# Positions of gathered rows dealt over groups of 8 partitions, and gathered rows turned by VectorE from the eleventh block on, in a mixture-of-experts decoder step

## The reference, cut to what matters

```python
T = 576; D_MODEL = 1024; N_EXPERTS = 64; TOP_K = 8; D_EXPERT = 256
s = sigmoid(h @ w_router); ...            # group-limited choice of 8 experts for each token
def step(acc, blk):                       # one block: up to 128 tokens
    e, tok, wt = blk
    xb = h[tok]
    hb = silu(xb @ we_g[e]) * (xb @ we_u[e])
    return acc.at[tok].add(wt[:, None] * (hb @ we_d[e]))
```

## Time and profile before

| | |
|---|---|
| median of 3 runs | 1124.86 us (1123.6 to 1125.34) |
| profiled execution, its own time | 1125.71 us |
| its span, first to last instruction | 1123.9 us |
| TensorE busy | 1092.7 us, 97% of the span |
| VectorE busy | 463.5 us, 41% |
| ScalarE busy | 236.7 us, 21% |
| GpSimd busy | 135.3 us, 12% |
| moved by DMA | 337.16 MB, mean 300 GB/s |

### The profile page before, as it was taken

One profiled execution on the slowest core, in us unless ns is written; L12 is line 12 of the kernel. 1 busy time (PEld: TensorE's weight loads), 2 busy tenths in 40 slices (PEclk: granted clock), 3 DMA queues, 4 the chain that ended last, 5 costly groups with the idle time before them and its releaser, 6 DMA issues.

```text
span 1123.9 us, 16923 instructions
## 1 busy us (share of the span) xinstructions
PE 1092.7 (97%) x6443; PEld 574.4 (51%) x6443; DVE 463.5 (41%) x1286; ACT 236.7 (21%) x516; POOL 135.3 (12%) x163
## 2 busy tenths in 40 slices
PE   6999999999999999999999999999999999999986
PEld 3456677777877544754343443443444444343332
DVE  2218541565456645843275233233233232231157
ACT  4131241223133223211111111111111111111111
POOL 0210000000020010121111112112111111111100
PEclk9999999999999999999999999999999999999999
DMA  9857622021170286789999999999999999999698
GB/s 371 325 201 302 227 79 75 1 85 34 80 255 18 91 286 229 273 302 403 418 425 424 423 417 426 422 415 398 424 411 379 422 408 392 415 395 370 222 415 341
DMA packets 51654, 337.16 MB, mean 300 GB/s; under 512 B 9636, under 2 KB 14088, under 8 KB 30830
## 3 DMA queue, kind: packets, MB, share of 16 engines
q1 hardware_dynamic: 33710, 287.32, 63.4%
q0 software_dynamic: 17856, 48.68, 11.7%
HBM read 311.30 MB, written 37.24 MB: 310 GB/s over the span
## 4 chain that ended last, share of the span: by engine, by line
PE 91%; DMA 4%; DVE 2%; ACT 1%; issue 1%; SPq 0%; DVEq 0%; POOLq 0%; ACTq 0%
PE bank L1565 30%; PE bank L1588 15%; PE bank L1261 10%; PE bank L1280 5%; PE bank L1553 4%; DMA mem<-expert_out_rows 3%; PE bank L1379 3%; PE bank L1174 3%; PE bank L1380 3%; PE bank L1497 3%; PE bank L1258 3%; PE bank L1149 1%; PE bank L1576 1%; PE bank L1344 1%; PE bank L1158 1%; PE bank L1132 1%
## 5 line engine op out<-in xcount | busy, mean ns | idle before, releaser
L1565 PE MATMUL bank<-mem 128*32 128x512 f32 (+2 forms) x1504 | 318.8, 594 | 0.6 <-DVE mem L2251 0.6
L1565 PEld LDWEIGHTS bank<-mem 128*32 128x32 f32 (+2 forms) x1504 | 106.7, 127 | 194.2 <-issue 194.2
L1588 PE MATMUL bank<-mem 128*32 128x512 f32 (+2 forms) x752 | 164.2, 596 | 1.1 <-ACT mem L1069 1.1
L2251 DVE COPY mem<-bank 128x512 f32<-128x512 f32 x48 | 33.2, 692 | 283.3 <-PE bank L1553 283.3
L1261 PE MATMUL bank<-hT,mem 128*128 128x288 f32 x512 | 133.3, 409 | 1.0 <-ACT mem L939 1.0
L1261 PEld LDWEIGHTS bank<-hT,mem 128*128 128x128 f32 x512 | 93.8, 190 | 25.8 <-issue 2.4
L1565 PE MATMUL bank<-x_sb,mem 128*32 128x512 f32 (+2 forms) x400 | 105.8, 593 | 0.0
L1588 PEld LDWEIGHTS bank<-mem 128*32 128x32 f32 (+2 forms) x752 | 51.7, 127 | 72.0 <-issue 71.1
L1069 ACT ACTIVATE mem<-bank 128x256 f32<-128x256 f32 x48 | 18.4, 384 | 313.0 <-PE bank L1576 312.8
L2266 DVE COPY hT<-bank 128x512 f32<-128x512 f32 x48 | 33.2, 692 | 85.4 <-PE bank L1588 85.4
L794 POOL DMA_INDIRECT mem<-ffn_in_rows,idxg x32 | 32.9, 1028 | 264.7 <-DVE idxs L2247 211.0
(11 more groups left out here) (400 smaller groups left out, 1279.3 us busy)
## 6 DMA issues: line engine op xcount, KB each, us to landing
mem<-k_w_exp SPq DMA_DIRECT2D x52, 2048.0 KB, 19.3
mem<-in_w_exp_down SPq DMA_DIRECT2D x52, 1024.0 KB, 20.6
x_sb<-k_w_exp SPq DMA_DIRECT2D x12, 2048.0 KB, 23.8
mem<-k_w_ada SPq DMA_DIRECT2D x8, 2048.0 KB, 9.3
mem<-k_w_in SPq DMA_DIRECT2D x7, 2048.0 KB, 9.4
hT<-in_w_exp_down SPq DMA_DIRECT2D x12, 1024.0 KB, 22.2
mem<-expert_out_rows SPq DMA_DIRECT2D x6, 2048.0 KB, 16.5
mem<-k_w_head SPq DMA_DIRECT2D x4, 2048.0 KB, 18.4
```

The lines of the kernel that those rows point to most:

```text
L1565: i = mm(bank[sl, :], xT[:, j % 2, c * BLK + sl.start:c * BLK + sl.stop], wview(r)[0][:, c, :], start=c == 0, stop=c == KC - 1)
L1588: i = mm(ps[4 + hf][sl, :], hhT[:, k * BLK + sl.start:k * BLK + sl.stop], wview(r)[1][:, k, hf * 512:(hf + 1) * 512], start=k == 0, stop=k ...
```

## The change

Two things change, and the order of some work with them.

**Dealing.** `deal` is a small table, written once, in place of `iota` in `slots_of`. For an expert part of k quarters (32k slots, 4k groups of 8 partitions) the position p goes to group p mod 4k, so that consecutive positions lie 8 slots apart, and the empty slots are the last of each group of 8 and no longer the end of the part. This holds for all blocks.

**Turning.** From block 10 on (the eleventh), TensorE's 8 transposes `x_T` and the two copies `xT_evac` go. VectorE transposes instead from the gathered rows in SBUF straight into `xT`, in 16 instructions for a block: each takes 32 partitions and 8 pieces of 32 columns and transposes each 32x32 square. 38 blocks (10 to 47) are turned in this way.

**Order.** From b = 9 on, `hh_T(b-1)` stands between the sixth and the seventh chunk of `up(b)` (so far only for b = 47). `up`, the gathers and some final waits ask for the semaphore `xT_ready`, which VectorE raises after its copy or its last transpose.

```diff
@@ slots_of (VectorE)
-                return stt(pm, p.to_broadcast([P, NT, w]), off, iota[:, 0:w].unsqueeze(1).to_broadcast([P, NT, w]),
+                return stt(pm, p.to_broadcast([P, NT, w]), off, dealt(w // QS).unsqueeze(1).to_broadcast([P, NT, w]),
                            ALU.add, ALU.is_equal)
@@ set-up (VectorE), DR = 8
+            for k in range(1, P // QS + 1):
+                cp(dealt(k).rearrange("p (e r) -> p e r", r=DR), iota[:, 0:k * QS].rearrange("p (r e) -> p e r", r=DR))
@@ VectorE
+            def turn(n, j, s=None):
+                g = gbuf(n, j)
+                dve.wait_ge(S[f"gat{g}"], gcount(n, j, s))
+                dve.wait_ge(S["eup"], n - 1)
+                rows = xg[g].rearrange("s (c d) -> s c d", c=KC)
+                cols = xT[:, j % 2, :].rearrange("d (c s) -> d c s", c=KC)
+                for q in range(P // QS):
+                    for a in range(P // QS):
+                        sl, dl = slice(q * QS, (q + 1) * QS), slice(a * QS, (a + 1) * QS)
+                        i = dve.transpose(cols[dl, :, sl], rows[sl, :, dl])
+                i.then_inc(S["xT_ready"], 1)
...
             for b in range(NBK):
                 if b + XG < NBK:
                     place(b + XG)
-                if b < NBK - 1:
+                if b + 1 < TURNED:
                     xT_evac(b + 1, b + 1)
+                elif b + 1 < NBK:
+                    turn(b + 1, b + 1)
                 gated(b, b)
@@ TensorE, TURNED = 10
-                if b < NBK - 1:
-                    up(b, b, pieces(b))
-                else:
-                    up(b, b, pieces(b), range(KC - 2))
+                split = KC if b + 1 < TURNED else KC - 2
+                up(b, b, pieces(b), range(split))
                 if b == 0:
                     pe.wait_ge(S["tab_ready"], 1)
                 else:
                     hh_T(b - 1)
-                if b == NBK - 1:
-                    up(b, b, pieces(b), range(KC - 2, KC))
-                if b < NBK - 1:
-                    x_T(b + 1, b + 1)
+                if split < KC:
+                    up(b, b, pieces(b), range(split, KC))
+                if b + 1 < TURNED:
+                    x_T(b + 1)
@@ GpSimd, before a gather
-                    pool.wait_ge(S["xgT_t"], n - XG + 1)
+                    pool.wait_ge(S["xT_ready"], n - XG + 1)
```

More of the change, by code:

```diff
@@ L39 @@
 QS = 32
+DR = 8
 NPRE = 3
@@ L50 @@
 XG = 3
+TURNED = 10
 OVMAX = 4 * U
@@ L192, in build @@
         n_out = sb("n_out", [(1 + NB) * H, DH])
+        deal = sb("deal", [P, 10 * QS], BF16)
         wtab = sb("wtab", [P, RQ])
@@ L488, in dn_count, with dealt @@
             return DN_LOADED[slot(r)][1] + 16 * loads_of(r)
+        def dealt(k):
+            return deal[:, k * (k - 1) // 2 * QS:k * (k + 1) // 2 * QS]
         def load_down(sp, dn, d, s):
@@ L649, in _ @@
             sp.wait_ge(S["eup"], max(LASTB[r] for r in range(NE) if slot(r) == XSLOT) + 1)
-            sp.wait_ge(S["xgT_t"], NBK)
+            sp.wait_ge(S["xT_ready"], NBK)
             for t in range(NT):
@@ L670, in _ @@
             overflow(sp, nov, body, last=last_rows)
-            sp.wait_ge(S["xgT_a"], NBK)
-            sp.wait_ge(S["xgT_d"], NBK)
+            sp.wait_ge(S["xT_ready"], NBK)
             for k in range(2):
@@ L1078, in body @@
                 silu(n, j)
-                xT_evac(n + 1, j + 1)
                 hhT_evac(n)
@@ L1097, in _ @@
             out_rows(NBK - 1, NBK - 1)
-            overflow(act, nov, body, lambda: xT_evac(NBK, NBK))
+            overflow(act, nov, body)
             for i, (t, _) in enumerate(COMBINE):
@@ L1541, in find_idx, with x_T @@
                 i.then_inc(S["idx_mm"], 1)
[L1543 to L1547, removed]
+            def x_T(n):
+                g = gbuf(n, n)
+                pe.wait_ge(S[f"gat{g}"], gcount(n, n))
+                if n:
                     pe.wait_ge(S["xgT_a"], n)
-                    pe.wait_ge(S["xgT_d"], n)
+                    pe.wait_ge(S["xT_ready"], n)
                 else:
@@ L1556, in up @@
             def up(n, j, parts, cs=range(KC)):
-                pe.wait_ge(S["xgT_a"], n + 1)
-                pe.wait_ge(S["xgT_d"], n + 1)
+                if isinstance(n, int) and n < TURNED:
+                    pe.wait_ge(S["xgT_a"], n + 1)
+                pe.wait_ge(S["xT_ready"], n + 1)
                 if not (isinstance(n, int) and n < 2):
@@ L1605, in body @@
                 up(n, j, whole)
-                x_T(n + 1, j + 1, s + 1)
                 find_idx(n + 2, j + 2, whole)
@@ L1620, in _ @@
             shared_up(KC // 2)
-            x_T(0, 0)
+            x_T(0)
             shared_up(2)
@@ L1651, in first_blocks @@
                 find_idx(NBK, NBK, whole)
-                x_T(NBK, 0, 0)
                 find_idx(NBK + 1, NBK + 1, whole)
             def last_done():
-                pe.wait_ge(S["xgT_a"], nov + (NBK + 1))
-                pe.wait_ge(S["xgT_d"], nov + (NBK + 1))
+                pe.wait_ge(S["xT_ready"], nov + (NBK + 1))
                 pe.wait_ge(S["ehh"], nov + NBK)
@@ L1665, in _ @@
             overflow(pe, nov, body, first_blocks, last_done)
-            for name in ("xgT_a", "xgT_d", "ehh", "ehT", "eout_a", "eout_d", "idx_ready"):
+            for name in ("xT_ready", "ehh", "ehT", "eout_a", "eout_d", "idx_ready"):
                 pe.wait_ge(S[name], NBK)
@@ L2270, in body @@
                 gated(n, j)
-                xT_evac(n + 1, j + 1)
+                turn(n + 1, j + 1, s + 1)
                 idx_out(n + 2, j + 2, s + 2)
@@ L2306, in first_blocks @@
                 place_more(NBK + 1, NBK + 1, 1)
-                xT_evac(NBK, NBK)
+                turn(NBK, 0, 0)
                 idx_out(NBK + 1, NBK + 1)
```

11 lines of the change are left out of this document (5 added, 6 removed).

## The result

The changed kernel takes 1134.45 us (median of 4 runs, 1133.96 to 1136.84), and before takes 1124.49 (4 runs, 1123.60 to 1125.34): ratio 1.0093, interval 1.0075 to 1.0110. It is 10 us slower. The forecast was 1123.5, and the range ended at 1131. The profiled execution took 1136.84 us, with a span of 1135.0.

The account below looks back on a forecast made before the run. TensorE, 97% busy, was taken to bound the kernel, with the DMA engines nearly full beside it. From 1124.86: -2 kept after loads give back most of -27.4, dealing 0, +0.6 for waits, giving 1123.5 us; range 1106 to 1131.

Parts of the forecast that it names:

- TensorE's list: Expert stage, blocks 10 to 47: TensorE loses `x_T`, its list 27.4 us shorter, 0.72 us a block.
- The term for the split of `hh_T`: `hh_T` in the middle of `up` costs TensorE 0.25 us a block, 9.5 us over 38 blocks.
- What the loads give back: Expert stage: TensorE soon waits for weight loads, so only 0 to -7 us of its gain is kept; -2 taken.
- Turning on VectorE: VectorE's 16 transposes a block take 0.40 us each, 6.4 us together, hidden within the block.
- Rival C: Turned blocks: VectorE becomes the bound if a transpose costs over 0.53 us; 1169 us at 0.6, 1224 at 0.69; chance 0.10.
- Gathers, GpSimd and the four copies: Gathers land in time, GpSimd waits for the turning instead, four small table copies are hidden: nothing added.
- Dealing: Expert stage: the new slot order acts only through the DMA engines, between +3 and -25 us; 0 taken.
- The sentence on the Trainium skill's swizzle: Partitions go to 16 DMA engines in runs of four, so dealt empty slots would all fall to every other engine.
- Crowding, +0.6: Waits that move gathers and loads against each other add about 0.6 us.
- rival D, +4: Expert stage: stops for loads, a lower clock behind some and more fully loaded engines cost +4 us, 1129; chance 0.13.
- Rival B, 1104,: Expert stage: dealing levels the DMA engines and loads land sooner, 21 us gained, 1104 us; chance 0.17.

Follow-up runs that it names:

- experiment 7: Changed kernel with the second half of each down-projection load left out from the twelfth expert on: 1099.07 us, 0.9770 of before.
- experiment 2: Kernel before with only the turning by VectorE from the eleventh block on, positions in their old order: 1128.77 us, 1.0031 of before.
- experiments 3, 5 and 11: Changed kernel with dealing over groups of 4 (1113.14 us); dealing over 8 turned round by 4 every second block (1111.66); no dealing, every second block reversed (1109.78).
- experiment 1: Kernel before with only the dealing over groups of 8, all blocks still turned by TensorE: 1133.68 us, 1.0089 of before.
- experiment 9: Changed kernel with unread matmuls (2, 5, 9, 6 and 9) ahead of the waits of blocks 17, 21, 33, 40 and 46: 1133.83 us, 1.0077 of before.
- Experiment 12: Changed kernel with the deal over 8 turned round by 4 in all blocks from the 25th on: 1120.11 us, 0.9956 of before.

## Why the prediction was wrong

**TensorE's list: right.** Predicted -27.4 us for 38 blocks, 0.72 each, 11.26 us a block. Measured 0.79 each, 11.13 a block (experiment 7), -29.3 in 37 blocks. The term for the split of `hh_T` was too large: `up` and `hh_T` take 811.73 - 804.45 = 7.28 us in block 27, against 7.19, 0.09 more and not 0.25; over the 37 blocks the 0.79 leave 0.97 - 0.79 = 0.18 on average.

**What the loads give back: the mechanism right, the sign and size wrong.** I wrote that TensorE begins to wait some four blocks into the turned ones, and that between 0 and 7 us are kept, and took 2. The first stop behind block 10's is at block 17, 2.4 us long, and the stops sum to 29.0. But it was wrong that the term can't be above 0. Turning alone costs +3.5 us (experiment 2): the loads did not land when they landed before. In this run's stage they move 407 GB/s, as the kernel before does:

```profile
600.00:1046.00 446.00, 423.88 (x2811) 153.04 (x2805) 362.68 (x940) 50.53 (x111) 74.69 (x73) 0.97 0.99 407
```

In before TensorE waits for nothing, so its 407 is what TensorE asked for. Here TensorE asks earlier and waits 22.1 us, and gets no more; with the engines level it gets 418 to 421 (experiments 3, 5 and 11).

**Turning on VectorE: right.** I took 0.40 us; it is 0.436, and it is hidden. Rival C is out. (Its times were a little high by its own terms: 13.1 - 11.98 = 1.12 us a block and not 1.15, so 1167.5 and not 1169, and 1222 and not 1224.) Gathers, GpSimd and the four copies were costed at nothing, and with half the down bytes gone (experiment 7) nothing else stops TensorE.

**Dealing: this is the step that failed.** I bounded it between +3 and -25 and took 0, "since a group of 8 keeps its full slots together at its start". The +3 was worked out from no row. It costs 10 us alone (1.0089, experiment 1) and about 7 on top of the turning (1.0093 against 1.0031). The sentence on the Trainium skill's swizzle had the right mechanism: by that rule the empty slots all fall to every other engine. I let it stand beside the sum and not in it, and I judged the damage by "the rest would be as loaded as the worst is now". The counts say that too: the fullest engine has 375 rows of the stage against 369 before. What changed is how many are that full: eight have 368 to 375 rows, against three above 345 before. The landing of the same pair of loads went from 18.5 to 26.1 us.

**Crowding, +0.6, and rival D, +4.** D named three things: stops, a lower clock behind them, and engines as loaded as the worst. The first and the last hold, the middle one was a small cost of its own if any, and the price was under half of the +10. By the rows the clock looks expensive. The blocks behind the five stops are longer than the same blocks of experiment 7 by 10.0 us in all, and the account closes: -29.3 of list, +29.0 of stops, and 10 of clock make the +10 of block 47's start. Yet experiment 9 gave the clock back at all five of them (it lost it again behind the new stop) and the time moved by 1.8 us (1.0077 for 1.0093), 5 at the most by the ends of the intervals. An account that adds up is not a cause: as far as this goes, the clock mostly decided how the waiting was divided. As the fillers may have cost time themselves, its price is bounded only loosely.

**Rival B, 1104,** was what dealing would have brought if it had evened the engines. With a deal that does, the gain is 12 to 15 us (1109.78 to 1113.14), and not 21.

So in order: TensorE's shorter list makes the loads the bound, and with unequal engines they land late. From 600 to the start of the last block the kernel with turning alone moves 404 GB/s in 450.2 us, the changed kernel 398 in 455.5 and the mirrored order 420 in 428.7. All three move 180 to 182 MB, so these rates are the times told in another way; what shows the cause is that only the order of slots differs between the runs. The changed kernel's last stretch before its last block, in the order of the table of stretches:

```profile
1046.00:1055.50 9.50, 9.50 (x58) 2.56 (x55) 0.61 (x2) 0.77 (x2) 0.00 (x0) 0.93 0.38 160
```

The share is 0.38 there: the queue runs empty. The last gate and up load is issued at 1030.72, when TensorE has done its part of block 45, lands 23.8 us later, at 1054.5, and the last block starts at 1055.48.

**Open.** Why eight engines at 368 to 375 rows are so much slower than one at 369 with the next at 364, 359 and 345. Experiment 12 points to lags within some blocks, but by my count the fullest engine's lead over the mean is about the same in both kernels (66 and 61 rows at block 40). Also open is how much of the fine difference between groups of 4, alternating and mirrored (0.9897, 0.9885, 0.9874) is real; the intervals overlap.

## What to carry to other kernels

Where DMA engines are at a share of 1, ask which of them carry the partitions that are empty: a share is a mean over 16, and an order of slots that spreads them within a block can pile them on half of the engines. Taking work from the co-bound engine pays nothing until that is level, and levelling pays nothing until the work is gone, so try the two together before dropping either. Check a price that closes an account (here the lower clock) by giving it back before believing it, with work that is surely shorter than the stop.

## What the runs showed of the hardware that was not expected

- Only the places of rows in a block, with the same bytes and the same TensorE list, move the landing of a 2 MB load by more than a factor of two near 933 us: 11.5, 18.5 or 26.1 us. The medians are 14.8, 19.3 and 23.4.
- Five different orders fit the rule of runs of four partitions: groups of 4 (0.9897), 8 (1.0093), 8 alternating (0.9885), 16 (1.0073) and mirrored (0.9874), each on the side that the count of rows says. The count itself is worked out, as said under **Theory**; only the times were measured.
- A float32 transpose of eight 32x32 blocks side by side takes 436 ns on VectorE (423 to 443), and they follow each other at 7.17 / 16 = 448 ns.
- Behind stops of 2.4 to 8 us TensorE runs at half of its clock for a while, and the block is 1.5 to 3.0 us longer; with matmuls in the stop it runs at the full clock from the first product (experiment 9, block 33).
- The most that any of these kernels moved over the stage from 600 to its last block is 421 GB/s.
